# The first eight modulation units as rows on TensorE in four column groups, with a new order of the first loads

## What is computed

```
mod_x = (silu(c) @ ada_w + ada_b)[:, None, :]      # c: 1 x 1024, ada_w: 1024 x 6144
mod_c = silu(c_ctx) @ ada_w + ada_b
sh1, sc1, g1, sh2, sc2, g2 = split(mod_x, 6)       # of mod_c only csh1 and csc1 are used
hx = rmsnorm(x, norm1_g) * (1 + sc1) + sh1
hc = rmsnorm(ctx, norm1_g) * (1 + csc1) + csh1
zx = hx @ w_in                                     # and hc @ w_in for keys and values
```

## Time and profile before

| | us |
|---|---|
| median of 3 runs | 1620.79 |
| lowest and highest | 1620.07, 1622.2 |
| the profiled execution's own time | 1615.77 |
| its span | 1614.0 |
| busy TensorE, VectorE, ScalarE, GpSimd | 1312.6, 922.6, 482.4, 284.5 |

### The profile page before, as it was taken

The page is one execution under the profiler, slowest core; times in us unless marked ns, Lnnn a source line. Parts: engine busy times, 40 slices in busy tenths (PEclk is TensorE's granted clock), DMA queues, the critical chain, the costliest instruction groups (busy, mean ns, idle before and its releaser), DMA issues. The chain is left out here.

```text
span 1614.0 us, 17696 instructions
## 1 busy us (share of the span) xinstructions
PE 1312.6 (81%) x6124; PEld 904.5 (56%) x6124; DVE 922.6 (57%) x1878; ACT 482.4 (30%) x1174; POOL 284.5 (18%) x294
## 2 busy tenths in 40 slices
PE   7998987998767856756756867877679998988996
PEld 3887655653223326646733633655459985746772
DVE  4865327667799846589879785544432634421001
ACT  2103312333323324334445542211132232522102
POOL 0120003334433332123222121211100000000000
PEclk9999989999999897977977678899989998999997
DMA  9991128999999998999999789999958664347883
GB/s 365 354 330 45 51 87 352 420 421 421 422 421 421 421 406 319 421 406 379 396 422 377 280 320 420 385 420 421 412 209 305 210 223 175 105 167 245 305 302 128
DMA packets 71987, 511.99 MB, mean 317 GB/s; under 512 B 8144, under 2 KB 8288, under 8 KB 10976
## 3 DMA queue, kind: packets, MB, share of 16 engines
q0 software_dynamic: 40400, 290.47, 44.4%
q1 hardware_dynamic: 30496, 216.77, 35.5%
q10 hardware_dynamic: 1008, 3.67, 0.7%
HBM read 509.83 MB, written 1.05 MB: 317 GB/s over the span
## 5 line engine op out<-in xcount | busy, mean ns | idle before, releaser
L928 PE MATMUL bank<-arena,diag 128*128 128x512 f32 x512 | 239.7, 618 | 60.4 <-ACT diag L1372 60.3
L953 PE MATMUL bank<-act_t,ring 128*128 128x128 f32 x2048 | 248.3, 282 | 27.6 <-DMA ring<-in_weights 21.7
L953 PEld LDWEIGHTS bank<-act_t,ring 128*128 128x128 f32 x2048 | 244.1, 199 | 47.3 <-issue 40.6
L1878 DVE SCALAR_TENSOR_TENSOR junk<-arena,bank 128x1024 f32<-128x1024 f32 x128 | 155.7, 1216 | 126.5 <-DMA arena<-in_experts,arena 126.4
L634 POOL DMA_INDIRECT arena<-in_experts,arena x128 | 129.6, 1013 | 444.7 <-DVE junk L1889 407.9
L928 PEld LDWEIGHTS bank<-arena,diag 128*128 128x128 f32 x512 | 96.5, 196 | 195.7 <-issue 110.0
L1872 DVE SCALAR_TENSOR_TENSOR junk<-arena,bank 128x1024 f32<-128x1024 f32 x128 | 154.2, 1220 | 65.6 <-DMA arena<-in_experts,arena 62.2
L610 POOL DMA_INDIRECT arena<-in_experts,arena x128 | 128.3, 1002 | 321.1 <-PE bank L928 174.1
L1889 DVE SCALAR_TENSOR_TENSOR junk<-arena,junk 128x1024 f32<-128x1024 f32 x127 | 162.6, 1280 | 4.6 <-ACT arena L1392 4.5
L963 PE MATMUL bank<-ring,act_t 128*128 128x256 f32 x576 | 131.4, 387 | 10.3 <-DMA ring<-in_weights 10.3
L1246 ACT ACTIVATE arena<-bank 128x512 f32<-128x512 f32 x74 | 43.5, 596 | 295.6 <-PE bank L963 68.2
(11 more groups left out here) (275 smaller groups left out, 1725.4 us busy)
## 6 DMA issues: line engine op xcount, KB each, us to landing
ring<-in_weights SPq DMA_DIRECT2D x201, 1024.0 KB, 6.6
arena<-in_ada_weights POOLq DMA_DIRECT2D x16, 1024.0 KB, 8.3
arena<-in_experts,arena POOLq DMA_INDIRECT x256, 14.6
row<-in_rows_in ACTq DMA_DIRECT2D x6, 512.0 KB, 3.8
arena<-in_ada_weights SPq DMA_DIRECT2D x2, 1024.0 KB, 11.3
arena<-in_rpb POOLq DMA_DIRECT2D x4, 512.0 KB, 15.1
res<-in_x SPq DMA_DIRECT2D x1, 1024.0 KB, 11.4
arena<-in_ctx_in SPq DMA_DIRECT2D x1, 1024.0 KB, 13.0
```

The source lines that it names most:

```text
L928: last = mm(bank(j), diag[:, k % 4, :], bufs[k % N_BUF][:, D + half * 512:D + half * 512 + 512], start=(k == 0), stop=(k == SLOTS - 1))
L953: last = mm(b[:, at + m * P:at + m * P + P], w[:, c, m * P:m * P + P], act_t[:, c, t * P:t * P + P], start=(c == 0), stop=(c == C - 1))
L1878: v.scalar_tensor_tensor(junk[:, 0, :], bufs1[k % N_BUF1][:, 0:D], 1.0, x_nat_at(1), ALU.mult, ALU.mult, accum_out=dots[:, 1, k:k + 1]).th ...
```

## The change

All eight first units become row jobs on TensorE, and come through the main ring. `silu_c` becomes 128 x 8 x 32: two real columns and thirty zeros for each c, zeroed by GpSimd ahead of the silu. The eight matmuls of a unit write to four groups of 32 output columns in turn (partitions 0, 32, 64 and 96 of the bank), so that a group takes two of them. ScalarE copies all 128 partitions, and the turn adds the four groups with `fold`, four stacked identities of 32, which moves from the late constants into the first (16 KB more at the start). VectorE's four early weighings and TensorE's sums of them go. The units before `w_in` in the main ring are eight instead of six. SP's first loads get a new order, and the second ring starts with the late units.

```
-ADA_ROW = (1, 3, 4, 5, 6, 7)
-ADA_EARLY = (0, 2)
-N_ADA = len(ADA_EARLY) + 16
+ADA_ROW = 8
+N_ADA = 16
...
-        silu_c = sb("silu_c", [P, C, 2])
...
+        silu_c = a1.take(C, 32)
+        ada_row = bias.rearrange("p t h c -> p (t h c)")[:, 0:ADA_ROW * 256]
...
+            def again(i, s):
+                sp.wait_ge(passed[s], i)
+                sp.dma_start(ring[s][:], weights[i * RING + s]).then_inc(loaded[s], 16)
 
             first(0)
-            first_ada(0)
             first(1)
             sp.dma_start(res[:], x.rearrange("(t p) d -> p t d", p=P)).then_inc(x_loaded, 16)
             first(2)
-            first_ada(1)
             first(3)
-            for s in range(2):
-                sp.wait_ge(passed[s], 1)
-                sp.dma_start(ring[s][:], weights[RING + s]).then_inc(loaded[s], 16)
+            for s in range(RING):
+                again(1, s)
+            again(2, 0)
+            again(2, 1)
+            sp.dma_start(ctx_nat, ctx_in.rearrange("(t p) d -> p t d", p=P)).then_inc(ctx_loaded, 16)
+            again(2, 2)
+            again(2, 3)
             sp.dma_start(row, rows_in[0:1, :].broadcast_to([P, D])).then_inc(row_loaded, 16)
-            sp.dma_start(ctx_nat, ctx_in.rearrange("(t p) d -> p t d", p=P)).then_inc(ctx_loaded, 16)
-            for s in range(2, RING):
-                sp.wait_ge(passed[s], 1)
-                sp.dma_start(ring[s][:], weights[RING + s]).then_inc(loaded[s], 16)
...
+            nc.gpsimd.memset(silu_c, 0.0).then_inc(silu_zero, 1)
...
-            for a in range(len(ADA_EARLY), N_ADA):
-                last = a - ADA_RING
-                if last >= 0:
-                    pool.wait_ge(weighted_ready, 2 * (last + 1) if last < len(ADA_EARLY) else
-                                 FIRST_WEIGHED + last - len(ADA_EARLY) + 1)
+            for a in range(N_ADA):
+                if a >= ADA_RING:
+                    pool.wait_ge(weighted_ready, a - ADA_RING + 1)
                 pool.dma_start(ada_ring[a % ADA_RING], ada_weights[a]).then_inc(ada_loaded[a % ADA_RING], 16)
-                if a == 9:
+                if a == 7:
...
                 for c in range(C):
-                    last = mm(b[0:2, 0:256], silu_c[:, c, :], w[:, c, :], start=(c == 0), stop=(c == C - 1))
+                    lo = 32 * (c % 4)
+                    last = mm(b[lo:lo + 32, 0:256], silu_c[:, c, :], w[:, c, :], start=(c < 4), stop=(c >= 4),
+                              skip_group_check=True)
...
                 for m in range(2):
-                    at = (2 * ADA_ROW[k] + m) * 2
-                    last = mm(b[:, at:at + 2], ada_row[:, k * 256 + m * P:k * 256 + m * P + P], ident[0:2, 0:2],
+                    at = (2 * k + m) * 2
+                    last = mm(b[:, at:at + 2], ada_row[:, k * 256 + m * P:k * 256 + m * P + P], fold[:, 0:2],
                               start=True, stop=True)
...
-            for k in range(len(ADA_ROW)):
+            for k in range(ADA_ROW):
                 ada_row_job(k)
                 if k:
                     ada_row_turn(k - 1, b)
-                if k == 3 or k == 5:
-                    e = k // 2 - 1
-                    for z in range(2):
-                        sum_weighted(2 * e + z, b, 4 * ADA_EARLY[e] + z, 2).then_inc(weighted_used, 1)
...
-                fn(ada_row[:, k * 256:k * 256 + 256], bank(j)[0:2, 0:256], ACT.Copy).then_inc(emptied[bank_of[j]], 1)
+                fn(ada_row[:, k * 256:k * 256 + 256], bank(j)[:, 0:256], ACT.Copy).then_inc(emptied[bank_of[j]], 1)
 
             take_row(0)
+            take_row(1)
             act.wait_ge(x_loaded, 16)
             sum_squares(0, res)
-            for k in range(1, len(ADA_ROW)):
+            for k in range(2, ADA_ROW):
                 take_row(k)
...
-            for a in range(len(ADA_EARLY)):
-                for z in range(2):
-                    weigh(2 * a + z, a, z)
-                if a == 0:
-                    norm(0, res, hat)
+            norm(0, res, hat)
```

More of the change, by code:

```diff
@@ L67 @@
 _n = 0
-for _name, _count in (("ada", 6), ("w_in", 8), ("band", 1), ("w_out", 4), ("wq", 8)):
+for _name, _count in (("ada", 8), ("w_in", 8), ("band", 1), ("w_out", 4), ("wq", 8)):
     UNITS[_name] = _n
@@ L105, in constants @@
 def constants():
-    first = np.zeros((P, 2 * P + GRID), np.float32)
+    first = np.zeros((P, 2 * P + GRID + 32), np.float32)
+    first[:, 2 * P + GRID:] = np.tile(np.eye(32), (4, 1))
     first[:, :P] = np.eye(P)
@@ L112, in constants @@
     inside = (col[None, :] >= c0[:, None]) & (col[None, :] < c0[:, None] + KW)
-    first[:, 2 * P:] = np.tile(np.where(inside, 0.0, NEG), (2, 1))
+    first[:, 2 * P:2 * P + GRID] = np.tile(np.where(inside, 0.0, NEG), (2, 1))
     second = np.zeros((P, N_CONST2), np.float32)
@@ L144, in constants @@
     put("level_mask", masks)
-    put("fold", np.tile(np.eye(32), (4, 1)))
     put("scan_keep", np.tile((np.arange(T) % 64 != 0).astype(np.float32), (P, 1)))
@@ L172, in build @@
         cols = sb("cols", [P, N_COLS])
-        c1 = sb("c1", [P, 2 * P + GRID])
+        c1 = sb("c1", [P, 2 * P + GRID + 32])
         mod = sb("mod", [P, 6, C, 2])
@@ L182, in build @@
         iota = c1[:, P:2 * P]
-        win_mask = c1[:, 2 * P:]
+        win_mask = c1[:, 2 * P:2 * P + GRID]
+        fold = c1[:, 2 * P + GRID:]
         ARENA = 36112
@@ L344, in build @@
         emptied = [sem(f"bank_emptied{b}") for b in range(8)]
-        ada_first_loaded = [sem(f"ada_first_loaded{s}") for s in range(len(ADA_EARLY))]
+        silu_zero = sem("silu_zero")
         ada_loaded = [sem(f"ada_loaded{s}") for s in range(ADA_RING)]
@@ L421, in sums @@
             jobs(name, n, HIGH)
-        sums("ada01", 1), jobs("ada_row", len(ADA_ROW)), jobs("x_t", 4)
+        sums("ada01", 1), jobs("ada_row", ADA_ROW), jobs("x_t", 4)
         for k in range(8):
@@ L554, in _ @@
             first(2)
[L555 removed]
             first(3)
[L557 to L566 removed]
+            for s in range(RING):
[5 more added lines that the diff above has]
+            again(2, 3)
+            sp.dma_start(row, rows_in[0:1, :].broadcast_to([P, D])).then_inc(row_loaded, 16)
+            with sp.Fori(3, N_UNITS // RING) as i:
                 for s in range(RING):
@@ L687, in sum_late @@
                 v = 2 + n // 4
-                last = sum_weighted(FIRST_WEIGHED + n, bank(JOB[f"ada{v}"]), 2 * (n % 4), 1)
+                last = sum_weighted(n, bank(JOB[f"ada{v}"]), 2 * (n % 4), 1)
                 if n % 4 == 3:
@@ L774, in _ @@
                     ada_row_turn(k - 1, b)
[L775 to L779 removed]
+            ada_row_turn(ADA_ROW - 1, b).then_inc(filled[bank_of[JOB["ada01"]]], 1)
             pe.wait_ge(hat_ready, 1)
@@ L1127, in second_block @@
                         last = mm(b[:, at:at + 32], own.cmp_rows[:, kv * 256 + m * P:kv * 256 + m * P + P],
-                                  const("fold"), start=True, stop=True)
+                                  fold, start=True, stop=True)
                 last.then_inc(filled[bank_of[j]], 1)
@@ L1259, in _ @@
             act.wait_ge(cols_loaded, 16)
+            act.wait_ge(silu_zero, 1)
             fn(silu_c[:, :, 0], colset("c"), ACT.Silu).then_inc(silu_ready, 1)
@@ L1635, in weighted_free @@
             def weighted_free(m):
-                if m >= 0 and m % 4 == 3:
+                if m % 4 == 3:
                     is_filled(dve, JOB[f"ada{2 + m // 4}"])
                 else:
-                    dve.wait_ge(weighted_used, FIRST_WEIGHED + (m + 1 if m < 0 else 3 * (m // 4) + m % 4 + 1))
+                    dve.wait_ge(weighted_used, 3 * (m // 4) + m % 4 + 1)
             def adaln_sum(n):
@@ L1734, in _ @@
                     evacuate_scaled("ctx_t", ctx_t, lambda c: scale_t[:, 1, c:c + 1], lambda c: mod[:, 0, c, 1:2])
-                weighted_free(n - 4)
-                weigh(FIRST_WEIGHED + n, len(ADA_EARLY) + n, 0)
+                if n >= 4:
+                    weighted_free(n - 4)
+                weigh(n)
                 if n >= 7 and n % 4 == 3:
@@ L2247 @@
     stages = {
-        "ada": [ada_units[u] for u in ADA_ROW], "w_in": column_units(a["w_in"][0]),
+        "ada": ada_units[:ADA_ROW], "w_in": column_units(a["w_in"][0]),
         "band": [band], "w_out": row_units_of(a["w_out"][0]),
@@ L2280 @@
     data = {
-        "weights": weights, "ada_weights": _np.stack([ada_units[u] for u in (*ADA_EARLY, *range(8, 24))]), "x": a["x"][0], "ctx_in": a["ctx"][0],
+        "weights": weights, "ada_weights": _np.stack(ada_units[ADA_ROW:]), "x": a["x"][0], "ctx_in": a["ctx"][0],
         "cols_in": _np.concatenate([as_column(small[n]) for n in COLS], 1),
```

16 lines of the change are left out of this document (4 added, 12 removed).

## The result

The kernel after takes **1610.44 us** (median of 11 runs, 1603.71 to 1617.21); the kernel before, run beside it, 1622.2 us (11 runs, 1612.9 to 1628.26). The ratio is **0.9933 (95% interval 0.9909 to 0.9957)**: 10.9 us faster, between 7.0 and 14.8 (the ratio on record is not the quotient of the two medians, which differ by 11.8 us). The profiled execution took 1608.12 us where that of before took 1615.77, a difference of 7.7 us.

What follows compares the result with a forecast made beforehand. The stretch from 40 to 134 us was taken as DMA-bound, ended by VectorE's chain from n = 9's landing. The only term, 1.96 us from the closed load gap, took 1620.79 to 1618.8 us, range 1615.0 to 1622.8.

Steps and rivals of the forecast that it cites:

- Nothing later is edited: Behind the first part: engines hand stages on in order, so its shift, 1.96 us, reaches the kernel's end at full size.
- Bytes decide: Loads from 40 to 97 us, DMA share 1.00: n = 9 lands once all bytes ahead have moved, 1.96 us sooner.
- The hole: DMA share falls to 0.44 between 36.5 and 40.0 us; closing it was to save 1.96 us.
- the prediction's own sign, n = 9 before 92 us: Weighing of n = 9 on VectorE: a start before 92 or after 98 us would show the argument from bytes wrong.
- full shift: Rival: GpSimd's issue times, not bytes, hold n = 9; it moves 7.0 us with the modulations, to 1613.8 us; chance 0.13.
- TensorE ready with the modulations at 29.8 to 31.1, `w_in` at 33 to 35: TensorE's start: row jobs follow the loads, so modulations are complete 5.7 to 7.0 us earlier than 36.8.
- if TensorE is still cold and a job late, the gain is 5: Modulations on TensorE: at the half clock and one job behind the landings, they come only 5 us earlier.
- The clock behind the wait: Rival at n = 15: TensorE arrives without waiting, band job avoids the half clock, 1.8 us more, 1617.0 us; chance 0.18.
- Mode switches at no cost: TensorE's row jobs: two switches a unit between column groups and whole array cost nothing that can be seen.
- ctx later: Start: ctx loads after two `w_in` units, landing near 38 us; n = 0 weighed at 41 to 42.4, 1.4 to 2.6 earlier.
- Crowding: Rival, loads at 31 to 60 us: ctx, `w_in` and late units collide, chain ends 3.9 us later, 1624.7 us; chance 0.09.
- no overlap: Rival, TensorE's row jobs: column groups run serially, eight units end 6.8 us late, up to 1627.6 us; chance 0.03.

Runs made afterwards that it cites:

- run 1: Kernel before with an unused tensor of 64 bytes a partition ahead of the statistics, shifting everything from `row` on: 1616.17 us, ratio 0.9949.
- 3: Kernel after with its eight row jobs plain (two stationary columns, whole array) instead of column groups: 1620.14 us, ratio 0.9995.
- 4: Kernel before with its six row jobs in four column groups, load order as before, arena placed as in the kernel after: 1611.53 us, ratio 0.9935.
- 7: Kernel after with the four `rpb` loads issued behind late unit n = 11 instead of n = 7: 1609.47 us, ratio 0.9921.
- run 8: Kernel after with one more unused 1 MB load, issued by SP just ahead of the row vector: 1612.04 us, ratio 0.9949.
- run 9: Kernel after with four extra unread column-group matmuls behind each of the first seven units, to keep TensorE busy: 1611.48 us, ratio 0.9942.
- run 10: Kernel after with GpSimd's mask add moved ahead of the issue of late unit n = 11: 1620.52 us, ratio 0.9988.
- 11: Kernel after with 24 unused bytes put in ahead of the late units' buffers in the arena: 1616.64 us, ratio 0.9957.
- 12: Kernel before with 64 unused bytes directly ahead of the arena, so `row` and `junk` stay in place: 1616.77 us, ratio 0.9964.
- Run 13: Kernel after with extra unread column-group matmuls on TensorE, four behind the first unit and twenty behind the second: 1613.02 us, ratio 0.9957.
- Run 2: Kernel after with its arena moved back by 64 bytes, to where it lay before: 1616.3 us, ratio 0.9954.
- run 5: Kernel after with the buffers behind the statistics moved 64 bytes further still: 1617.75 us, ratio 0.998.
- 6: Kernel after with the buffers behind the statistics moved 128 bytes further still: 1617.52 us, ratio 0.9971.

## Why the prediction was wrong

**"Nothing later is edited", so the shift passes on at full size: failed, and it is the largest error.** The step put everything behind the first 134 us at nothing: the sum has 1.96 us in all, 10.9 were measured, and 4.3 us (the tile in the profiles) to 5.4 us (the ratios) of them arise there. The shift did pass on, as far as the profiles show: 3.7 us at the attention and 3.9 at the first dot in the first pair, 5.6 and 4.8 in the means of all profiles with either start (below). But the edit of a buffer's home changed the addresses behind it, and with them the rate of the gathers in another stage (421 to 427 GB/s in the page). All kernels of this study sort by this alone. At +64 bytes (after twice, 1, 3, 4, 7 to 13) the tile takes 318.1 to 319.6 us; at 0 (before twice, 2), +128 (5) and +192 (6) it takes 322.5 to 323.7. In the second expert tile, whose gathers go to buffers in the same arena, DMA moves 421 GB/s between 1040 and 1120 us at the three bad places and 424 or 425 at the good one, but that tile's length does not sort by it (first to last dot 570 to 578 us against 564 to 579). Why the place is good is open: alignment to 128 bytes was tried and fell.

The ratios say the same. With their means in bold:

| | place of before or another bad one | +64 bytes |
|---|---|---|
| code of before | 1, 1.0004: **1.0002** | 0.9949, 0.9964: **0.9957** |
| code of after | 0.9954, 0.9980, 0.9971: **0.9968** | 0.9933, 0.9948, 0.9957: **0.9946** |

The place is worth 0.45% in the one row and 0.22% in the other, 0.34% or 5.4 us in the mean; the profiles say 4.3 to 5. The code is worth 0.34% and 0.11%, 0.22% or 3.6 us in the mean. Each single ratio has an interval of about 0.2% to either side, so the split is rough: taken from the quotients of the medians, place and code come out at 0.27% each, 4.4 us. Over both rows together each is clear of zero; which is the larger is not settled.

**"Bytes decide" for n = 9: failed as a sum, right as one part.** The hole closed as forecast, and the sum took 1.96 us for it and nothing else. But n = 9 moved by 3.7 us in the first pair, and by 5.5 in the means of all profiles with either start. (By the prediction's own sign, n = 9 before 92 us, the argument would have passed at 93.5; the sign was too wide.) Two things add up to it. The first is when GpSimd issues `rpb`, and behind it the unit of n = 8: 2.33 us earlier in the first pair, 2.8 in the means. That issue hangs on the weighing of n = 4, which stands behind ctx's transposes on TensorE, and those behind the first `w_in` jobs. Two runs show that this is not the bytes: in run 1 the first `w_in` jobs started 0.9 us later and took 15.53 us instead of 14.05, and the issue came at 68.9 instead of 66.8, with the same 25.1 MB moved until then; in run 8 0.8 MB more had been moved, and the issue was not later. So the rival "full shift" was right in this part. The second is the time from that issue to the start of n = 8. Before, then after (length, PEclk, DMA share, GB/s):

```profile
66.81:92.28 25.47, 1.00 1.02 299
64.48:88.86 24.38, 1.00 1.01 291
```

That part is bytes. In all sixteen profiles that issue `rpb` behind n = 7 the share in this stretch is 1.01 or 1.02, at 285 to 311 GB/s. Ten of them move 6.9 to 7.1 MB in it and take 22.8 to 24.5 us; six move 7.3 to 8.9 MB and take 24.2 to 29.6, and all four with before's start are among these six (7.6, 8.9, 7.3 and 7.8 MB). The prediction took the same loads to be ahead in both kernels; what the half MB more is that lands there ahead of n = 8 is open. So a DMA share of 1.00 priced the length of the wait rightly; what it did not say is what starts it.

**TensorE ready with the modulations at 29.8 to 31.1, `w_in` at 33 to 35: failed in size.** The step was "if TensorE is still cold and a job late, the gain is 5". It was cold throughout: 1.93 + 1.01 us for each unit, last turn over at 32.4, transposes at 3.65 instead of 1.97. The prediction had the cold unit at 3.0 us, more than the 2.56 between landings, and did not add up the lateness. The modulations gained 4.4 us (32.4 for 36.8), and the cold transposes took 1.7 of them back. So `w_in` moved by 2.94 us and not by 5 to 7, and past 37 us, the prediction's own sign that its argument on TensorE was wrong. That is why the full shift did not give its 7 us either. The Trainium skill (TensorE: Matmul & The Clock Gate, HAM oscillation) describes work whose wait for the next data is longer than the work itself, so that every piece starts at the low clock. Run 13 agrees that waits bring the fall, from 1.04 to 1.93 us a job behind waits of 1.57 and 0.42 us. The kernel after differs: its last wait for a landing is before 14.64 us, and the six jobs from there on are at the half clock without one. What keeps it there is not shown.

**The clock behind the wait:** did not occur in the first pair, but did in four of the six profiles with after's start. In the first profile of the kernel after, TensorE never waited at n = 1 or n = 9 (57.00 us busy of 57.00 from 40 to 97), came to n = 15 with 1.23 us of wait, and the band job took 5.39 us as before. In runs 2, 5, 6 and 11 TensorE is delayed, not by waiting but by the clock: the first `w_in` jobs take 15.4 to 16.0 us instead of 14.05. Then it comes to n = 15 with no wait, the band job takes 3.70 us, and the attention starts at 139.1 to 139.6 instead of 140.7 and 142.3. (The second profile of the kernel after has the slow first jobs too, 15.47 us, but n = 9 later by 1.1 us, and waits 1.52 us at n = 15.) Run 2, the last sums and the band job:

```profile
129.02 1.84 PE L681 MATMUL bank<-arena 128*128 128x1 f32 x16
130.73 3.70 PE L811 MATMUL bank<-ring,arena 128*128 128x256 f32 x16
```

Over all seventeen profiles the band job takes 3.70 us where TensorE waited 0.41 us or not at all before the last sum (eight profiles), and 5.25 to 6.75 behind waits of 1.23 to 3.31 (eight; the one exception is run 9, 3.70 behind 1.73). Before's start has both kinds too (run 1 and before's second profile at 3.70), so how much of the change's gain this is can't be told.

**Mode switches at no cost: no cost seen.** The turn at 11.47 starts before the job of 9.60 is over (9.60 + 1.93 = 11.53). The ends of matmuls are modelled in these records, so a cost below some 0.1 us would not show. **ctx later, the collision of n = 13 moving along: right** (n = 0 at 41.4 against a forecast of 41 to 42.4). That VectorE's early weighings are worth nothing by themselves was not tried alone. **Crowding and no overlap:** did not occur; the DMA share of 1.01 at 36.5 to 40 speaks against the one, 1.93 us a job against the other.

**The sum.** 3.7 us at the start and 4.3 to 4.6 in the tile make 8.0 to 8.3; the table of ratios gives 9.0 (3.6 + 5.4). The measured 10.9 us has an interval from 7.0 to 14.8, which holds both, and the second measurement of the same kernel gave 8.4 us (0.9948). The start may be worth more than the first pair of profiles shows: the four profiles with the start of before (before twice, 1 and 12) reach the attention at 144.4, 148.8, 142.9 and 146.8, mean 145.7; the six with that of after (after twice, 2, 5, 6 and 11) at 139.1 to 142.3, mean 140.1. That would be 5.6 us; at the first dot of tile 1 the same means are 269.0 and 264.2, 4.8 us apart. Single profiles of the same start differ by up to 6 us, so this part is not settled closer than 3.6 to 5.6.

## What to carry to other kernels

A buffer that is added, dropped or moved shifts every address behind it: list which later buffers move, and before giving a gain or a loss to the edit, run the old kernel with a pad that makes the same shift. Cut both profiles at marks and compare stage by stage, because a total hides that half of it comes from a stage that nobody edited. Profile each kernel more than once before reading a difference of a few us off one pair: here the same start put the attention anywhere in a range of 6 us, while the gathers' stage repeated to 1.5 us. And a DMA share of 1.00 says that the queues are full, not who releases the transfer that ends last: follow its issue back first, and price in bytes only what lies behind that issue.

## What the runs showed of the hardware that I had not expected

- **A shift of the arena changes the rate of indirect gathers into it by 1.4%**: 421 against 427 GB/s over the stage, 322.5 to 323.7 us (five profiles) against 318.1 to 319.6 (twelve) for 128 gathers, from 64 bytes in each partition; one of four places tried is good.
- **GpSimd's add of 128 x 4096 holds up more than one kind of operation on VectorE**: a `tensor_scalar` of 0.35 us took 6.68 beside it (run 10), where in the earlier trace rows it was the seven `scalar_tensor_tensor` that took 12.38 for 3.62.
- **The clock record can miss the first 40 us**: in the kernel after the stretch from 2.4 to 36.5 us shows 1.00, while its column-group jobs took 1.93 us, which is the half clock of the earlier trace rows. In run 5 the jobs have the same durations and the record shows the half clock, in the row below (length, PEclk, DMA share, GB/s). The durations tell the level there.

```profile
30.00:36.50 6.50, 0.50 1.01 405
```
